# Two key units per place: a sample's logits and value products in pairs among the network's products

## What is computed

```python
# attention of the sample over its paged cache (8 heads x 64), per sample
k_past = cache_k[page_table]; v_past = cache_v[page_table]      # 64 pages of 128 positions
s = q . k * 64**-0.5 + qc - kc                                  # kc: forget terms
att = softmax(s) @ v
# ConvFFN of the prompt and of the sample
h  = x1 @ w_up + b_up
hc = b_conv + causal depthwise conv of width 3 over positions of h
out = (gelu(hc_gate) * hc_val) @ w_down
x2 = LayerNorm(alpha * x1 + out) * ln2_g + ln2_b
```

## Time and profile before

| | us |
|---|---|
| median of 3 runs | 3110.25 |
| lowest and highest run | 3105.86, 3114.26 |
| the profiled execution: span, first to last instruction | 3104.8 |
| its own time beside the span | not given apart; the median is 5.4 above the span |
| PE busy | 2980.9 (96%) |
| DVE, ACT, POOL busy | 2011.5, 1554.0, 810.0 |
| joint stage, from its first product to the end of its last | 1186.6 to 3014 |
| mean TensorE clock granted | 0.981 of full |

### The profile page before, as it was taken

How to read it: one execution, slowest core, us unless ns; L and a number is a source line. 1 busy time by engine, 2 the same in 40 slices (tenths; PEclk the granted TensorE clock), 3 DMA queues, 4 the chain that set the end, 5 groups by cost and what they waited for, 6 DMA issues and landing times. The chain is left out here.

```text
span 3104.8 us, 57063 instructions
## 1 busy us (share of the span) xinstructions
PE 2980.9 (96%) x19424; PEld 2376.2 (77%) x19424; DVE 2011.5 (65%) x4185; ACT 1554.0 (50%) x3113; POOL 810.0 (26%) x1437
## 2 busy tenths in 40 slices
PE   8999978999999997999999999999999999999988
PEld 8999966777777886777777777777777777777762
DVE  5433336787886655866678666678666678666445
ACT  3111115776775113466445666446676446766424
POOL 1101110000000103434444334454343454442300
PEclk9999988999999998999999999999999999999999
DMA  5444455322303356757877677787677887775868
GB/s 205 134 127 122 127 133 152 81 55 67 86 21 112 122 166 219 253 197 247 289 270 262 235 247 246 268 298 269 222 245 230 284 299 240 249 240 177 301 249 323
DMA packets 270120, 626.51 MB, mean 202 GB/s; under 512 B 52279, under 2 KB 116695, under 8 KB 261855
## 3 DMA queue, kind: packets, MB, share of 16 engines
q1 hardware_dynamic: 169271, 305.32, 30.9%
q0 software_dynamic: 93760, 296.83, 28.2%
q10 hardware_dynamic: 6800, 20.71, 2.1%
HBM read 555.52 MB, written 67.33 MB: 201 GB/s over the span
## 5 line engine op out<-in xcount | busy, mean ns | idle before, releaser
L1568 PE MATMUL F_ps_u<-X_x_hi,F_w_hi 128*128 128x512 f32 x1408 | 577.4, 410 | 10.9 <-DVE F_w_lo L1827 10.9
L1569 PE MATMUL F_ps_u<-X_x_lo,F_w_hi 128*128 128x512 f32 x1408 | 560.0, 398 | 0.0
L1570 PE MATMUL F_ps_u<-X_x_hi,F_w_lo 128*128 128x512 f32 x1408 | 559.8, 398 | 0.0
L1827 DVE TENSOR_TENSOR F_w_lo<-X_raw,F_w_hi 128x512 fp32r<-128x512 f32 x352 | 239.2, 681 | 269.9 <-ACT F_w_hi L1727 268.2
L2056 POOL DMA_DIRECT2D N_dec<-cache_k x512 | 278.1, 543 | 312.5 <-issue 192.9
L2096 POOL DMA_DIRECT2D N_dec<-cache_v x512 | 281.9, 551 | 285.0 <-issue 163.7
L1568 PEld LDWEIGHTS F_ps_u<-X_x_hi,F_w_hi 128*128 128x128 f32 x1408 | 266.7, 189 | 103.5 <-issue 34.9
L1727 ACT CAST F_w_hi<-X_raw 128x512 fp32r<-128x512 f32 x352 | 214.3, 609 | 256.0 <-PE F_ps_y L1570 230.8
L1884 DVE STREAM_TRANSPOSE N_dec<-N_dec 128x1024 f32<-128x1024 f32 x256 | 303.6, 1222 | 19.2 <-DMA N_dec<-cache_k 18.8
L1570 PEld LDWEIGHTS F_ps_u<-X_x_hi,F_w_lo 128*128 128x128 f32 x1408 | 266.3, 189 | 64.5
L1569 PEld LDWEIGHTS F_ps_u<-X_x_lo,F_w_hi 128*128 128x128 f32 x1408 | 267.3, 190 | 56.7
(11 more groups left out here) (345 smaller groups left out, 6388.3 us busy)
## 6 DMA issues: line engine op xcount, KB each, us to landing
N_dec<-cache_k POOLq DMA_DIRECT2D x512, 256.0 KB, 3.6
N_dec<-cache_v POOLq DMA_DIRECT2D x512, 256.0 KB, 4.7
X_raw<-w_up_t SPq DMA_DIRECT2D x120, 512.0 KB, 5.2
F_raw<-w_up_t SPq DMA_DIRECT2D x56, 512.0 KB, 5.0
X_raw<-w_down SPq DMA_DIRECT2D x56, 512.0 KB, 5.4
sc_qk<-A_early SPq DMA_DIRECT2D x16, 1024.0 KB, 5.1
F_forget<-sc_wT POOLq DMA_DIRECT2D x256, 64.0 KB, 3.0
F_raw<-w_down SPq DMA_DIRECT2D x32, 512.0 KB, 4.3
```

What stands on the lines that cost most here:

```text
L1568: nc.tensor.matmul(out, a_hi, b_hi, start=first, stop=False)
L1569: nc.tensor.matmul(out, a_hi, b_lo, start=False, stop=False)
L1570: return nc.tensor.matmul(out, a_lo, b_hi, start=False, stop=last)
L1827: nc.vector.tensor_tensor(w_lo[:, q % 4, :], raw[q // 2 % RAW][:, q % 2 * 512:(q % 2 + 1) * 512], w_hi[:, q % 4, :].bitcast(F32), ALU.subt ...
```

## The change

Logits and value products of two units are done in one place. `decode_places` goes over pairs of units: for samples 1 to 7 a pair has T, E, T, E, QV, K on six places (eight in up parts, where a pair begins at a multiple of four), for sample 0 Q, R, K and an empty place, for the last values T, E, T, V. There is a second kt buffer, a second pt, and the second unit's logits go to the half of the PSUM bank that the transposes use. K is a new step: DVE turns the second unit's keys there, and POOL issues two halves. kin keeps its three half buffers. Where the loads are issued changes: values at QV and V, ahead of bias and keys, four more halves before the loop. To make room, the rows of gain and shift move into chunks of g (loaded by SP at the start of each later block) and, for the last stage, over the sample's buffers; ids moves beside vnew.

```diff
@@ decode_places
-            names = ("Q", "R") if s == 0 else ("T", "E", "QV") if s < NB else ("T", "V")
-            for u in range(UN):
+            if s == 0:
+                names = (("Q", 0, 0), ("R", 0, 0), ("K", 0, 0), None)
+            elif s < NB:
+                names = (("T", -1, 0), ("E", -1, 0), ("T", -1, 1), ("E", -1, 1), ("QV", 0, 0), ("K", 0, 0))
+            else:
+                names = (("T", -1, 0), ("E", -1, 0), ("T", -1, 1), ("V", -1, 0))
+            for u in range(0, UN, 2):
                 if 0 < s and is_up(q):
                     q += -(q % HB) % 4
...
-        kt = persist["dec"][:, 3072:5120].rearrange("p (a b) -> p a b", a=16)
+        kt = [persist["dec"][:, 3072:5120].rearrange("p (a b) -> p a b", a=16), persist["dec"][:, 13376:15424].rearrange("p (a b) -> p a b", a=16)]
...
-        pt, ptn = m.sb("pt", [P, 2, 4, 32]), m.sb("ptn", [32, 2, 32])
+        pt, ptn = m.sb("pt", [P, 2, 2, 4, 32]), m.sb("ptn", [32, 2, 32])
...
-        ps_s, ps_o = ps_t[:, 2 * P:4 * P], ps_d[:, 0:2 * P]
+        ps_s, ps_o = [ps_t[:, 2 * P:4 * P], ps_t[:, 0:2 * P]], ps_d[:, 0:2 * P]
@@ sync
-            sp.dma_start(gain[:, :], io["ln2_g"].partition_broadcast(P).rearrange("p a d -> p (a d)")).then_inc(norm.rows_in, 16)
-            sp.dma_start(shift[:, :], io["ln2_b"].partition_broadcast(P).rearrange("p a d -> p (a d)")).then_inc(norm.rows_in, 16)
             for q in range(NQ):
                 b, i, f, gv, hf = where(q)
+                if b and i == 0:
+                    sp.wait_ge(g_lo_done, SWEEPS * FC * b)
+                    for row, name in ((gain, "ln2_g"), (shift, "ln2_b")):
+                        sp.dma_start(row, io[name].partition_broadcast(P).rearrange("p a d -> p (a d)")).then_inc(norm.rows_in, 16)
...
             sp.wait_ge(att_out, NB)
+            for row, name in ((persist["gain2"], "ln2_g"), (persist["shift2"], "ln2_b")):
+                sp.dma_start(row[:, :], io[name].partition_broadcast(P).rearrange("p a d -> p (a d)")).then_inc(persist["gain2_in"], 16)
             load_sample(0)
@@ tensor
             def turn_p(s, u):
...
-                pe.wait_ge(s_copied, min(UN * (s + 1) + u, NK))
+                pe.wait_ge(s_copied, min(UN * (s + 1) + u - u % 2, NK))
...
             def qk(s, u):
                 n = UN * s + u
                 pe.wait_ge(k_turned, 2 * n + 2)
-                if n:
-                    pe.wait_ge(s_copied, n)
+                if n >= 2:
+                    pe.wait_ge(s_copied, n - 1)
                 if s:
-                    pe.wait_ge(t_copied, part(s - 1, u) + 1)
+                    pe.wait_ge(t_copied, part(s - 1, u - u % 2 + 1) + 1)
...
                     if kind in ("Q", "QV"):
                         qk(s, u)
+                        qk(s, u + 1)
                     if kind == "QV":
                         times_v(s - 1, u)
+                        times_v(s - 1, u + 1)
                     if kind == "V":
                         times_v(s, u)
+                        times_v(s, u + 1)
@@ scalar
-                    if kind == ("E" if s < NB - 1 else "V") and u + 1 < UN:
+                    if kind == "E" and u + 1 < UN:
                         exp(s, u + 1)
+                    if kind == "V" and u + 2 < UN:
+                        exp(s, u + 2)
@@ vector
+                    if f == GAIN:
+                        dve.wait_ge(norm.gained, TPB * b)
...
             def turn_k(n):
                 for half in (2 * n, 2 * n + 1):
                     dve.wait_ge(k_in[half % KR], 32 * (half // KR + 1))
-                    if n:
-                        dve.wait_ge(s_done, n)
+                    if n >= 2:
+                        dve.wait_ge(s_done, n - 1)
...
             def add_forget(s, u):
...
-                dve.wait_ge(s_done, n + 1)
+                dve.wait_ge(s_done, n - n % 2 + 2)
...
             turn_k(0)
+            turn_k(1)
             for q in range(NQ):
...
                     if kind in ("R", "QV"):
                         add_forget(s, u)
-                        if u < UN - 1:
-                            turn_k(UN * s + u + 1)
-                        if u == UN - 1:
+                        add_forget(s, u + 1)
+                        if u == UN - 2:
                             ends(s)
-                            if s + 1 < NB:
-                                turn_k(UN * s + u + 1)
-                    if kind == "V" and u == UN - 1:
+                        if UN * s + u + 2 < NK:
+                            turn_k(UN * s + u + 2)
+                    if kind == "K" and UN * s + u + 3 < NK:
+                        turn_k(UN * s + u + 3)
+                    if kind == "V" and u == UN - 2:
                         ends(NB)
@@ gpsimd
             for n in range(2):
                 load_v(n)
+            for half in range(KR, KR + 4):
+                load_k(half)
...
-                    if kind == "Q":
-                        load_k(2 * n + 3)
-                        load_k(2 * n + 4)
-                    if kind == "T":
-                        coming = n + UN
-                        for half in (2 * coming + 3, 2 * coming + 4):
+                    if kind in ("QV", "V"):
+                        done = n - UN if kind == "QV" else n
+                        for v in (done + 2, done + 3):
+                            if v < NK:
+                                load_v(v)
+                    if kind in ("Q", "QV"):
+                        for coming in (n + 2, n + 3):
+                            if coming < NK:
+                                load_bias(coming)
+                        for half in (2 * n + 7, 2 * n + 8):
                             if half < 2 * NK:
                                 load_k(half)
-                        if n and n + 1 < NK:
-                            load_v(n + 1)
-                    if kind in ("Q", "QV"):
-                        if n + 2 < NK:
-                            load_bias(n + 2)
...
+                    if kind == "K":
+                        for half in (2 * n + 9, 2 * n + 10):
+                            if half < 2 * NK:
+                                load_k(half)
```

More of the change, by code:

```diff
@@ L1337, in invert, with scale_rows @@
         link(nc.vector.tensor_tensor(inv, inv, t1, ALU.mult))
-    def scale_rows(self, dve, link, halves, k):
+    def scale_rows(self, dve, link, halves, b, k):
         nc = self.nc
-        dve.wait_ge(self.rows_in, 32)
+        dve.wait_ge(self.rows_in, 32 * (b + 1))
         for w, row in enumerate(halves):
@@ L1375, in decode_places @@
         for s in range(NB + 1):
-            names = ("Q", "R") if s == 0 else ("T", "E", "QV") if s < NB else ("T", "V")
-            for u in range(UN):
+            if s == 0:
[5 more added lines that the diff above has]
+            for u in range(0, UN, 2):
                 if 0 < s and is_up(q):
                     q += -(q % HB) % 4
-                for name in names:
-                    at[q] = (name, s if name in ("Q", "R", "QV") else s - 1, u)
+                for entry in names:
+                    if entry:
+                        at[q] = (entry[0], s + entry[1], u + entry[2])
                     q += 1
@@ L1398, in stage_ffn_decode @@
         ident, snew, attT_s = persist["ident"], persist["snew"], persist["attT_s"]
-        gain, shift = persist["gain2"], persist["shift2"]
+        GAIN = LATE - 4
+        gain, shift = (persist["g"][:, f:f + 2, :].rearrange("p f t -> p (f t)") for f in (GAIN, GAIN + 2))
         norm = BlockNorm(nc, m, TPB, gain, shift, persist["stats"], persist["mv"], persist["inv"])
@@ L1616, in qk @@
                 for st in range(2):
-                    out = ps_s[:, st * P:(st + 1) * P]
+                    out = ps_s[n % 2][:, st * P:(st + 1) * P]
                     for half in range(2):
@@ L1620, in qk @@
                             f = 2 * (4 * st + hs) + half
-                            last = nc.tensor.matmul(out[32 * hs:32 * hs + 32, :], qbd[:, f, :], kt[:, f, :],
+                            last = nc.tensor.matmul(out[32 * hs:32 * hs + 32, :], qbd[:, f, :], kt[n % 2][:, f, :],
                                                     start=half == 0, stop=half == 1, skip_group_check=True)
@@ L1631, in times_v @@
                         row = 64 * st + 32 * (b % 2)
-                        last = nc.tensor.matmul(ps_o[row:row + 32, :], pt[:, st, b, :],
+                        last = nc.tensor.matmul(ps_o[row:row + 32, :], pt[:, u % 2, st, b, :],
                                                 vin[:, n % 2, b, st * 2 * P:(st + 1) * 2 * P], start=u == 0 and b == 1,
@@ L1874, in measure, with scale_rows @@
                 norm.moments(rows[w][:, k, :], w, k)
-            def scale_rows(k):
-                norm.scale_rows(dve, norm_links, [x[:, k, :] for x in rows], k)
+            def scale_rows(b, k):
+                norm.scale_rows(dve, norm_links, [x[:, k, :] for x in rows], b, k)
             def turn_k(n):
@@ L1888, in copy_pt @@
```

(6 more changed lines are left out.)

16 lines of the change are left out of this document (9 added, 7 removed).

## The result

The changed kernel takes 3583.69 us (median of 4 runs, 3574.45 to 3585.91), the kernel before beside it 3112.26 (4 runs): ratio 1.1516, 95% interval 1.1497 to 1.1534. It is slower by 15%, as forecast (3579). The profiled execution took 3574.45 with a span of 3572.7, against 3104.8: 467.9 more.

What follows compares the result with a forecast made beforehand. PE bounds the joint stage (busy 368.3 of 370 us). Up pairs 300, down pairs 164, other pairs -5 and the start +10 give +469; with span 3104.8 and 5.4 to the median, 3579 us, range 3270 to 3700.

Steps and rivals of the forecast that it cites:

- part 1: PE's trips to logits and values: 72 fewer, each sparing 0.33 us paid for going there and back, 24 us in all.
- landing of it: Second transfer of key half 2n+7, behind 2 MB of V: lands 4.0 us after issue, at 17.2 after the logits.
- stall, down: Down pairs: PE stands 7.4 us at place 4 for g_lo, which DVE makes only after the late key turn.
- stall for w_lo, up: Up pairs: PE waits 4.0 us for w_lo of place 5, made only after the late key turn.
- stall for the exponents, up: Up pairs: the second T, at place 6, waits 3.3 us for ACT's exponents, themselves behind a DVE convolution.
- slow products, down pair: PE's low clock after a down stall costs 2.0 us a pair, bounds 1.5 and 3.0.
- slow products, up pair: PE's low clock after up stalls, the first slow stretch partly covered: 1.0 us a pair, bounds 0 to 1.5.
- 1 (faster): Rival: neither wait reaches PE and only the spared trips and the start count, 3096 us; needs the half landed by 9.8; 5%.
- Rival 2: Keys come in time and only ACT's chain shows, 37 x 1.6 = 59 us more: 3155 us; chance 5%.
- Rival 3: PE's lead is larger than read, so only what DVE can't catch up counts: 3276 us; chance 15%.
- Rival 4: Eight V transfers in a row slow POOL or the landing by 2 to 5 us: 3690 to 3860 us; 7%.
- Rival 5: The second unit in a place gains nothing, the rest as forecast: 3603 us; chance 2%.

Runs made afterwards that it cites:

- keys_first: Against the changed kernel, GpSimd issues the two key halves of the QV step ahead of values and forget terms: 3233.25 us, ratio 1.0389.
- keys_first_spaced: keys_first with, in up parts, an empty place between E and the second T: 3168.69 us, ratio 1.0186.
- one_key_start: Against one_key_first, halves 2 to 6 are fetched before the first two V, first two turns moved into the loop (places 1, 3): 3152.02 us, ratio 1.0128.
- late_turn: Against the changed kernel, from sample 1 VectorE turns half 2n+7 at the next T, not at K: 3310.39 us in one run.
- spaced: Against the changed kernel, up pairs of samples 1 to 7 run T, E, empty, T, E, empty, QV, K: 3555.6 us in one run.
- one_key_first: Against keys_first_spaced, GpSimd issues half 2n+7 first, then the forget terms, V, and half 2n+8 last: 3166.47 us, ratio 1.0174.
- start_late: Against one_key_start, VectorE turns half 2n+7 at the next pair's first T, not at K (first sample's pairs but the last unchanged): 3114.61 us, ratio 1.0012.
- start_late_wide: Against start_late, the layout with an empty place after E covers every pair beginning in an up part: 3094.52 us, ratio 0.9954.

## Why the prediction came out right

| step of the prediction | forecast | measured |
|---|---|---|
| part 1, per spared excursion | 0.33 us | 0.33 (26.73 against 27.06) |
| excursion to the next product | 3.6 | 3.61 (1569.57 to 1573.18) |
| second key transfer out, after the logits | 13.2 | 13.2 |
| landing of it | 4.0 | 3.2 (turn at 16.4, not 17.2); median of 55 pairs 3.1 |
| stall, down | 7.4 | 6.46; mean of F_g_lo 95.1/15 = 6.3 |
| stall for w_lo, up | 4.0 | (136.5-15.6-6.9)/33 = 3.5 |
| stall for the exponents, up | 3.3 | 82.2/37 = 2.2 |
| the T's wait without the key wait | 1.6 | 1.60 (keys_first) |
| slow products, down pair | 2.0 | 1.9 |
| slow products, up pair | 1.0 | 1.8 |
| down pair with clock | 30.4 | 30.4 (median of 16) |
| up pair with clock | 35.0 | 34.1 (mean of 28) |
| PE goes on at the start | 1211.7 | 1212.78 |
| X places | nothing | 23.6 for mxe |

The mechanism is the predicted one, and keys_first shows it: the bottleneck is one key half (two transfers of 256 KB) that goes out 13 us after the logits and would have to land by 9.8. The places are right too: 33 waits for w_lo and 37 for the exponents (38 up pairs forecast), 19 for g_lo (18 down pairs).

**Two sizes were off and cancelled.** The forecast had 420 us of stalls, 74 of clock and 24 spared. Measured are 353.5 us of standing and 114.4 of longer busy time, in which some 23 are spared: so about 137 for the clock and what else a stall adds to busy time. The stalls are 67 too high, though 24 for mxe were not foreseen, and the clock is up to 63 too low (38 by the count of slow products below). By the table the stalls came out some 20 us shorter in the down pairs, 19 at w_lo and 42 at the exponents. The first two follow the landing, for which I took 4.0 "near its own median" of before, with 2 MB of V ahead of it. The page gives these medians for all transfers of the changed kernel:

```profile
N_dec<-cache_k POOLq DMA_DIRECT2D x512, 256.0 KB, 3.2
N_dec<-cache_v POOLq DMA_DIRECT2D x512, 256.0 KB, 3.7
```

Before they were 3.6 and 4.7; the half on the path landed in 3.1. The 2.6 that I worked out from the Trainium skill, "DMA: Bandwidth & Descriptors", section "Anatomy of one DMA — SWDGE (gpsimd) path", lies below the median of all these kernels. That the clock made up for the landing is luck; a forecast within 5 us of the result is closer than its terms were. The exponents and the clock are a different case, as the next paragraphs show: there the same time stood in the other column.

**The clock term.** After a down stall (changed kernel, timeline of PE, one in three products shown):

```profile
1725.15 0.77 PE L1579 MATMUL F_ps_y<-F_w_hi,F_g_hi_h 128*128 128x512 f32 x1 [8.14 <-DVE F_g_lo_h L1855]
...
1726.57 0.63 PE L1579 MATMUL F_ps_y<-F_w_hi,F_g_hi_h 128*128 128x512 f32 x1
...
1727.85 0.63 PE L1579 MATMUL F_ps_y<-F_w_hi,F_g_hi_h 128*128 128x512 f32 x1
...
1729.13 0.63 PE L1579 MATMUL F_ps_y<-F_w_hi,F_g_hi_h 128*128 128x512 f32 x1
...
1730.27 0.48 PE L1579 MATMUL F_ps_y<-F_w_hi,F_g_hi 128*128 128x512 f32 x1
```

Three products take 1.28 us instead of 0.70 (granted clock 0.50, 1.2 GHz), and the place takes 5.12 where it took 2.94 with its T: 2.2 lost, near the 2.0 of the sum. (The kernel before has such a stall too, which the prediction passed over: 6.95 us at 1186.59, after which twelve products take 5.3 us instead of 2.8.) In up pairs there are two patterns:

```profile
1419.83 0.79 PE L1579 MATMUL F_ps_u<-X_x_hi,F_w_hi 128*128 128x512 f32 x1 [2.62 <-DVE F_w_lo L1843]
...
1422.55 0.63 PE L1579 MATMUL F_ps_u<-X_x_hi,F_w_hi 128*128 128x512 f32 x1
...
1429.73 0.44 PE L1615 MATMUL F_ps_t<-all_ident,F_ecur 128*128 128x128 f32 x2 [1.24 <-ACT F_ecur L1784]
...
1939.66 0.50 PE L1579 MATMUL F_ps_u<-X_x_hi,F_w_hi 128*128 128x512 f32 x1 [2.63 <-DVE F_w_lo L1843]
...
1941.17 0.40 PE L1579 MATMUL F_ps_u<-X_x_hi,F_w_hi 128*128 128x512 f32 x1
...
1948.22 0.69 PE L1615 MATMUL F_ps_t<-all_ident,F_ecur 128*128 128x128 f32 x2 [2.67 <-ACT F_ecur L1784]
```

At 1419.83 six products take 2.72 us, at 1.2 GHz, and PE then stands only 1.24 for the exponents. At 1939.66, after the same stall, six take 1.51, at 2.4 GHz; PE stands 2.67 for the exponents, and it is the products behind that stall that are slow, three in 1.42. The first pattern is the rule: products run slow behind 28 of the 33 waits for w_lo, and 25 of the 37 waits for the exponents are 1.61 or less. In the other five pairs that wait is 2.67. So some 1.1 us of each slow stretch are covered by a shorter wait for the exponents; the prediction said "partly covered", took 1.0 for the clock and left the wait at 3.3. In a pair it is 2.2 and 1.8: 4.0 together against 4.3 forecast.

Counted over the stage (distances of more than 0.36 us between the starts of two products, less 0.234), 591 slow products cost 121 us, against 43 and 9 us in the kernel before: 112 of the 137. Of the 121, 50 stand behind the waits for w_lo and 19 behind those for the exponents, 1.8 a pair; 36 stand behind the waits for g_lo, 1.9 each; 16 behind others. Of the 25 us that remain, some 15 are an estimate for the last product before each of 94 more stalls, which counts with its 0.39 us and not with 0.23; the rest isn't taken apart. By the Trainium skill, "TensorE: Matmul & The Clock Gate", section "HAM oscillation — how this bites in real kernels", such a loop starts cold in every turn; by this trace that holds behind 17 of the 19 waits for g_lo and 28 of the 33 for w_lo, and in the five other up pairs behind the second stall.

**The step that was missing.** X1 follows the last K of a sample at once, and DVE makes mxe there. The prediction followed the K of a pair up to the next pair, and not up to the X places. This didn't decide in the changed kernel (23.6 us). The repaired ones, where I counted the regular pairs and the start and took everything else for nothing, came out 78 and 71 above the 3155 and 3098 expected. The X places are one part of that: in keys_first_spaced 14.4 us of waits, beside 36 for g_lo, exponents at seams and V, with low clock behind part of them. In one_key_start PE stands some 56 us in 24 waits (those over 0.9 us) in the stage behind its first products, against 13 us in 7 in the kernel before. These 43 us and 12 more of slow products outweigh the 23 spared.

Of the rivals, 1 (faster) named the right condition: the half must land 9.8 us after the logits. In the changed kernel it lands at 16.5 in the median. Issued first (keys_first) it lands at 8.9, yet later than 9.8 in 16 of 55 pairs, and DVE still stands for it. Rival 2 at 3155 supposed the keys in time; the kernel that does this, keys_first, is 3233. Rival 3 (what DVE can't catch up) is out: the stalls come from a single late hand-over in each pair, with DVE busy for 56% of the span. Rival 4 is out by the landings, which got no longer. Rival 5 (3603) the time alone could hardly tell from the forecast; what rules it out is that already in the changed kernel the pairs of sample 0 take 13.32 us, against 2 x 6.82 before.

**Still open.** A fourth half buffer, which would let the half start a whole place earlier, wasn't tried. late_turn and spaced are single runs. What the forget terms in one_key_first would be worth without the keys' later landing isn't known.

## What to carry to other kernels

When work is merged into bigger steps, list for each buffer what frees it and behind what its refill stands in the issuing engine's queue: here the saving was 0.33 us a pair, and the price of one half behind twelve other transfers was 7 to 9. Put first in a queue what is due first, and ask for it last; each of the two edits alone took 270 us or more off the changed kernel. And don't judge an edit by the wait that it removes, but by what the engine on the path then stands: one_key_first took away 71 us of DVE's waits, 67 came back under other names, and nothing was gained; start_late took 31 us of waits off PE itself, with 9 us of slow products behind them, and gained 36.

## What was not expected of the hardware

- Stalls of the same length had different sequels. In the up pairs of the changed kernel, waits for w_lo of 2.43 to 2.94 us were followed by products at 1.2 GHz in eight cases and at 2.4 GHz in four. All 30 waits of about 1.6 us for the exponents in keys_first left the clock at its upper level. So a single stall says little about the price of its kind; the count over the trace does.
- A median over all transfers of a line hid the one that mattered. The page's landing of the keys is 3.6 us before, 3.2 in the changed kernel, 4.0 in keys_first and 4.9 in start_late_wide. The second transfer of half 2n+7 landed in 3.0 to 3.1 in the median in all of the versions with two units in a place but late_turn, whether V went out ahead of it or behind. What lengthened the page's median are above all the halves issued at K, whose second transfers took 6.0 to 6.6 in the versions with a key half first and 3.4 to 4.8 in the changed kernel. In late_turn, with POOL's order as in the changed kernel, it was 5.5; why is not shown.
